# Both feed-forward blocks multiply by Strassen's scheme, with weight and token sums on VectorE

## The reference

```python
def swiglu(h, w_gate, w_up, w_down):
    return (jax.nn.silu(h @ w_gate) * (h @ w_up)) @ w_down

x = x + g2 * swiglu(modulate(rms_norm(x, norm_ffn[i]), sh2, sc2),
                    ffn_w_gate[i], ffn_w_up[i], ffn_w_down[i])     # i = 0, 1
```

## Time and profile before

| | before |
|---|---|
| median of 3 runs, us | 3224.8 |
| lowest and highest run, us | 3221.25, 3227.31 |
| profiled execution, us | 3226.9 |
| TensorE busy | 3013.9 us, 93% |
| VectorE, ScalarE, GpSimd busy | 1004.6, 646.0, 1067.1 us |
| matmul records in the gate and up products, two blocks | 1408 |
| matmul records in the down products, two blocks | 704 |

### The profile page before, as it was taken

One profiled execution on the slowest core, in us unless ns is written; L12 is line 12 of the kernel. 1 busy time (PEld: TensorE's weight loads), 2 busy tenths in 40 slices (PEclk: granted clock), 3 DMA queues, 4 the chain that ended last, 5 costly groups with the idle time before them and its releaser, 6 DMA issues.

```text
span 3226.9 us, 27822 instructions
## 1 busy us (share of the span) xinstructions
PE 3013.9 (93%) x10207; PEld 1660.1 (51%) x10207; DVE 1004.6 (31%) x2078; ACT 646.0 (20%) x1454; POOL 1067.1 (33%) x574
## 2 busy tenths in 40 slices
PE   7899999999999999997888969999999999999997
PEld 5455555476656644654556555444444444444443
DVE  6333455304455523335444164100000222100001
ACT  2132233113333412313322122100000100100000
POOL 5781681086460018608800000582000780000000
PEclk7899999989999999998889989999999999999999
DMA  7341341253321024313200101343222452222222
GB/s 240 103 127 62 114 126 45 85 147 85 85 79 33 27 83 121 103 59 108 72 17 26 52 1 39 122 156 96 71 75 78 140 159 65 78 78 71 73 72 71
DMA packets 267621, 278.07 MB, mean 86 GB/s; under 512 B 39379, under 2 KB 240352, under 8 KB 267392
## 3 DMA queue, kind: packets, MB, share of 16 engines
q1 hardware_dynamic: 238528, 175.56, 18.0%
q0 software_dynamic: 28224, 100.86, 10.2%
q10 hardware_dynamic: 768, 0.30, 0.0%
HBM read 274.59 MB, written 2.10 MB: 86 GB/s over the span
## 4 chain that ended last, share of the span: by engine, by line
PE 86%; DVE 7%; ACT 2%; DMA 2%; issue 2%; POOL 1%; SPq 1%; DVEq 0%; ACTq 0%; POOLq 0%
PE psum L683 44%; PE psum L831 10%; PE psum L1283 9%; PE psum L1118 2%; PE psum L710 2%; PE psum L805 2%; PE psum L1149 2%; PE psum L1104 2%; PE psum L725 2%; PE psum L817 1%; PE psum L1154 1%; PE psum L955 1%; PE psum L956 1%; DVE probs L2022 1%; DVE row_max L1988 1%
## 5 line engine op out<-in xcount | busy, mean ns | idle before, releaser
L683 PE MATMUL psum<-h,ring 128*128 128x512 f32 (+1 forms) x3216 | 1393.7, 594 | 33.4 <-ACT h L1416 27.3
L683 PEld LDWEIGHTS psum<-h,ring 128*128 128x128 f32 x3216 | 617.5, 194 | 771.8 <-issue 757.1
L610 POOL DMA_DIRECT2D ada_ring<-in_ada_w x192 | 115.1, 599 | 1574.7 <-DVE gains L1907 1361.4
L622 POOL TENSOR_SCALAR ada_ring<-ada_ring,cond 128x1024 f32<-128x1024 f32 x168 | 479.3, 2853 | 9.5 <-POOL ada_sum L626 1.8
L626 POOL TENSOR_TENSOR ada_sum<-ada_sum,ada_ring 128x1024 f32<-128x1024 f32 x168 | 394.9, 2350 | 14.9
L831 PE MATMUL psum<-og,ring 128*128 128x512 f32 x768 | 333.1, 593 | 2.3 <-DVE og L2440 2.0
L1283 PE MATMUL psum<-arena,ring 128*128 128x512 f32 x704 | 302.5, 592 | 0.0
L831 PEld LDWEIGHTS psum<-og,ring 128*128 128x128 f32 x768 | 144.6, 190 | 181.8 <-issue 178.3
L1283 PEld LDWEIGHTS psum<-arena,ring 128*128 128x128 f32 x704 | 133.8, 190 | 168.4 <-issue 168.4
L2450 DVE TENSOR_TENSOR arena<-psum,arena 128x512 f32 x44 | 30.4, 691 | 573.7 <-PE psum L683 573.7
L2069 DVE SCALAR_TENSOR_TENSOR x<-psum,mods,x 128x512 f32<-128x512 f32 x64 | 48.0, 751 | 481.9 <-PE psum L1283 272.2
(11 more groups left out here) (294 smaller groups left out, 2752.2 us busy)
## 6 DMA issues: line engine op xcount, KB each, us to landing
ada_ring<-in_ada_w POOLq DMA_DIRECT2D x192, 512.0 KB, 4.0
ring<-in_ffn_w_gate SPq DMA_DIRECT2D x22, 1024.0 KB, 5.3
ring<-in_ffn_w_up SPq DMA_DIRECT2D x22, 1024.0 KB, 5.3
ring<-in_ffn_w_down SPq DMA_DIRECT2D x32, 704.0 KB, 4.6
ring<-in_sc_w_in SPq DMA_DIRECT2D x12, 1024.0 KB, 6.6
ring<-in_mla_w_in SPq DMA_DIRECT2D x10, 1024.0 KB, 6.2
ring<-in_mla_w_out SPq DMA_DIRECT2D x8, 1024.0 KB, 5.2
ring<-in_swa_w_in SPq DMA_DIRECT2D x16, 512.0 KB, 5.3
```

What stands on the lines that cost most here:

```text
L610: pool.dma_start(ada_ring[:, i % 2, :], w[k * P:(k + 1) * P, first(part)]).then_inc(arrived[i % 2], n.give(f"ada_in{i % 2}", 16))
L622: step = nc.gpsimd.tensor_scalar(piece, ada_ring[:, i % 2, :], c, None, ALU.mult)
L683: m = pe.matmul(tile.at[:, part], lhs(k), rhs(k), start=(k == 0), stop=(k == K - 1))
```

## The change

Both blocks multiply by Winograd's form of Strassen's scheme. In a product each operand is seen as 2 x 2 quarters: the weights a11, a12 (the second half of the summed features), a21 (the second 128 output features), a22 (both), the tokens b11, b12 (the later 256 tokens), b21 (the second half of the summed features), b22 (both). Seven products of half width, called p1 to p7, take the place of eight:

- p1 = a11 b11, p2 = a12 b21, p6 = s2 t2, p5 = s1 t1, p7 = s3 t3, p3 = s4 b22 and p4 = a22 t4, in the order in which TensorE runs them (`first_parts`, `other_parts`). s1 to s4 are four sums of weight quarters, t1 to t4 four of token quarters. Each part is m accumulating matmuls of 128x128 by 128x256; m is 4 for gate and up, and 4, 4 and 3 for the three chunks into which the hidden tiles are cut for the down product.
- The parts of a slot go into three banks, and several of them build on one another in a bank. Between them ScalarE copies what a bank holds (`snaps`, after p1, p6 and p5) and VectorE adds such a copy and a bank (after p2, p7 and p3). For the down product VectorE adds each partial result straight to x, seven times a chunk (`add_chunk`).
- VectorE makes the sums of weights for each slot from the ring (`sum_weights`, four tensor_tensor of 128x(128 m)), once its transfer has landed and before TensorE comes to the slot's third part. It makes the token sums once a block for h (four of 128x1024) and once for each of the three chunks of hidden tiles.
- The down weights are loaded as 12 slots of 2m x 256 columns instead of 16 of 11 x 128.
- The order at the block's start: the first two slots do p1 and p2 both before the other parts of either, slot_begun comes at the second slot's p6, and the last `result_squares` before a block gives one slot_begun more so that both slots are loaded. `add_result` of the layer before makes the first slot's sums ahead of its last tile.

```diff
+HALF = T // 2
+BANK_SETS = ((0, 1, 3), (5, 6, 7))
+DOWN_CHUNKS = ((0, 4), (8, 4), (16, 3))
+PARTS_DONE = ((1, 2, 3, 4, 5, 6, 7), (8, 9, 10, 11, 12, 13, 14))
+FIRST_PARTS_DONE = ((1, 2, 5, 6, 7, 8, 9), (3, 4, 10, 11, 12, 13, 14))
...
-                    halves = [down[s * 11 * P:(s + 1) * 11 * P].rearrange("(k p) n -> p k n", p=P) for s in range(2)]
-                    for c in range(KT):
-                        for s in range(2):
-                            load((lambda slot: slot[:, 0:11 * P].rearrange("p (k n) -> p k n", n=P),
-                                  halves[s][:, :, c * P:c * P + P]))
+                    for pair in range(KT // 2):
+                        for first, m in DOWN_CHUNKS:
+                            load((lambda slot: slot[:, 0:2 * m * 256].rearrange("p (k n) -> p k n", n=256),
+                                  rows_of(down)[:, first:first + 2 * m, 256 * pair:256 * pair + 256]))
...
+                added = pe.matmul(SB[0], ones, sq_sum[:, :], start=True, stop=False, skip_group_check=True)
+                if frees_slot:
+                    added.then_inc(S["slot_begun"], n.give("slot_begun"))
...
+            def part(out, weights, moving, m, begins, slot_begins=False, fresh=None):
+                for k in range(m):
+                    if fresh is not None:
+                        pe.wait_ge(S["h_ready"], fresh + k + 1)
+                    last = pe.matmul(out, weights[:, k, :], moving[:, k, :], start=begins and k == 0, stop=True,
+                                     skip_group_check=True)
+                    if k == 0 and slot_begins:
+                        last.then_inc(S["slot_begun"], n.give("slot_begun"))
+                last.then_inc(S["part_done"], n.give("part_done"))
...
+            def first_parts(c, slot_begins=True, fresh=None):
+                b11, b12, b21, b22 = c.moving
+                part(c.banks[0], c.a11, b11, c.m, True, slot_begins=slot_begins, fresh=fresh)
+                part(c.banks[2], c.a12, b21, c.m, True, fresh=None if fresh is None else fresh + c.m)
+            def other_parts(c, moving_ready=None, slot_begins=False):
+                b11, b12, b21, b22 = c.moving
+                t1, t2, t3, t4 = c.sums
+                s1, s2, s3, s4 = c.w
+                pe.wait_ge(S["weights_summed"], n.take("weights_summed"))
+                if moving_ready is not None:
+                    pe.wait_ge(S["moving_summed"], moving_ready)
+                pe.wait_ge(S["snap_read"], c.snapped(1))
+                part(c.banks[0], s2, t2, c.m, False, slot_begins=slot_begins)
+                part(c.banks[1], s1, t1, c.m, True)
+                pe.wait_ge(S["snap_read"], c.snapped(2))
+                part(c.banks[0], s3, t3, c.m, False)
+                pe.wait_ge(S["snap_read"], c.snapped(3))
+                part(c.banks[1], s4, b22, c.m, False)
+                if moving_ready is not None:
+                    pe.wait_ge(S["moving_summed"], moving_ready + 1)
+                pe.wait_ge(S["sum_read"], c.summed(2))
+                part(c.banks[0], c.a22, t4, c.m, False)
...
             def ffn(job):
...
+                chunks = [Chunk(open_slot(), 4, i, moving, moving_sum, lambda k, i=i: snap0 + 4 * i + k,
+                                lambda k, i=i: sum0 + 3 * i + k) for i in range(2)]
+                first_parts(chunks[0], slot_begins=False, fresh=h0)
+                first_parts(chunks[1], slot_begins=False)
+                other_parts(chunks[0], moving_ready=t0 + 3)
+                other_parts(chunks[1], slot_begins=True)
...
+                with turns(pe, FT // 2 - 1, n, {"slot_full0": 16, "slot_full1": 16, "slot_begun": 2, "part_done": 14,
+                                                "weights_summed": 2, "snap_read": 7, "sum_read": 7}):
+                    snap_at, sum_at = n.of["snap_read"], n.of["sum_read"]
                     for i in range(2):
...
+                for pair in range(KT // 2):
+                    for at, (first, m) in enumerate(DOWN_CHUNKS):
+                        i = (3 * pair + at) % 2
+                        snap_at, sum_at = n.of["snap_read"].at, n.of["sum_read"].at
+                        pe.wait_ge(S["snap_read"], snap_at - 3)
+                        pe.wait_ge(S["sum_read"], sum_at - 4)
+                        if pair == 0:
+                            pe.wait_ge(S["hid_ready"], hid0 + (first + 2 * m) // 2)
+                        hid = ffn_hid[:, first:first + 2 * m, :]
+                        t2, t3, t4 = [v[:, 0:m, :] for v in hid_sum[at]]
+                        c = Chunk(open_slot(), m, i, halves_of(hid, m), (hid[:, 0:m, late], t2, t3, t4),
+                                  lambda k: snap_at + k, lambda k: sum_at + k)
+                        first_parts(c)
+                        other_parts(c, moving_ready=t0 + 4 * at + 3 if pair == 0 else None)
...
+                def turn(parts_done):
+                    at, summed = n.of["part_done"], n.of["sum_read"]
                     for i in range(2):
-                        tile = next_tile()
-                        done(tile)
-                        nc.scalar.activation(ffn_sig[:, i, :], tile.at, ACT.Silu).then_inc(tile_used[tile.bank], 1)
-                    skip(2)
-                squares_of_result()
+                        p1, p2, p6, p5, p7, p3, p4 = parts_done[i]
+                        r1, r2, r3 = [psum[:, b, early] for b in BANK_SETS[i]]
+                        for snap, (part, bank) in enumerate(((p1, r1), (p6, r1), (p5, r2))):
+                            act.wait_ge(S["part_done"], at.now(part))
+                            nc.scalar.activation(snaps[i][snap], bank, ACT.Copy).then_inc(S["snap_read"], n.give("snap_read"))
+                        if i == 0:
+                            act.wait_ge(S["sum_read"], summed.now(2))
+                            nc.scalar.activation(ffn_sig[:, 1, late], ffn_sig[:, 1, late], ACT.Silu)
+                            act.wait_ge(S["sum_read"], summed.now(3))
+                            nc.scalar.activation(ffn_sig[:, 0, :], ffn_sig[:, 0, :], ACT.Silu)
+                            act.wait_ge(S["part_done"], at.now(p4))
+                            nc.scalar.activation(ffn_sig[:, 1, early], r1, ACT.Silu).then_inc(S["snap_read"], n.give("snap_read"))
...
+            def sum_weights(i, m, steps=range(4)):
+                p = weight_slot[0] % 2
+                if 0 in steps:
+                    dve.wait_ge(S[f"slot_full{p}"], n.take(f"slot_full{p}", 16))
+                a11, a12, a21, a22 = quarters_of(ring[:, p], m)
+                s1, s2, s3, s4 = sums_of(weight_sum[i], m)
+                for step in steps:
+                    if step == 0:
+                        nc.vector.tensor_tensor(s1, a21, a22, ALU.add).then_inc(S["dve_step"], n.give("dve_step"))
+                    elif step == 1:
+                        nc.vector.tensor_tensor(s3, a11, a21, ALU.subtract)
+                    elif step == 2:
+                        dve.wait_ge(S["dve_step"], n.now("dve_step"))
+                        settle(nc.vector.tensor_tensor(s2, s1, a11, ALU.subtract))
+                    else:
+                        nc.vector.tensor_tensor(s4, a12, s2, ALU.subtract).then_inc(S["weights_summed"],
+                                                                                   n.give("weights_summed"))
+                        weight_slot[0] += 1
...
+            def first_weights_of(job):
+                weight_slot[0], n.of["slot_full0"].at, n.of["slot_full1"].at = MARK["ffn", job]
+                sum_weights(0, 4)
...
+            def gated_pair(hid, parts_done, between, first=False):
+                at, snapped = n.of["part_done"], n.of["snap_read"]
+                for i in range(2):
+                    p1, p2, p6, p5, p7, p3, p4 = parts_done[i]
+                    r1, r2, r3 = [psum[:, b, early] for b in BANK_SETS[i]]
+                    put = hid if i else [ffn_sig[:, q, :] for q in range(2)]
+                    if first and i == 0:
+                        sum_weights(1, 4)
+                    if not first and i == 0:
+                        dve.wait_ge(S["hid_ready"], n.now("hid_ready"))
+                    dve.wait_ge(S["part_done"], at.now(p2))
+                    dve.wait_ge(S["snap_read"], snapped.now(4 * i + 1))
+                    nc.vector.tensor_tensor(put[0][:, early], r3, snaps[i][0], ALU.add).then_inc(S["sum_read"], n.give("sum_read"))
+                    if i or not first:
+                        sum_weights(1 - i, 4)
+                    dve.wait_ge(S["part_done"], at.now(p7))
+                    dve.wait_ge(S["snap_read"], snapped.now(4 * i + 3))
+                    nc.vector.tensor_tensor(put[1][:, late], r1, snaps[i][2], ALU.add).then_inc(S["sum_read"], n.give("sum_read"))
+                    dve.wait_ge(S["part_done"], at.now(p3))
```

(64 more changed lines are left out.)

132 lines of the change are left out of this document (92 added, 40 removed).

## The result

The changed kernel takes 3148.3 us (median of 4 runs, 3146.9 to 3154.2) against 3223.9 before (4 runs beside them, 3221.3 to 3227.3): a ratio of 0.9765, 95% interval 0.975 to 0.9779. That is 75.6 us less; the forecast was 68 less, 3157 us. The spans of the profiled executions differ by 81.0: 3226.9 and 3145.9.

The account below looks back on a forecast made before the run. The number and width of TensorE's passes were taken to bound the feed-forward blocks. The terms -109 + 23 + 12.8 + 2.5 + 3 = -68 us took 3224.8 to 3157 us, range 3118 to 3200 (0.81).

Parts of the forecast that it names:

- The products: Feed-forward matmuls: 1848 half-width passes a block at 0.2157 us, 401.4 us with slow start, saving 109 us over both blocks.
- The rival of unhidden loads: TensorE's weight loads in series add at most 0.149 us to each of 3696 passes: 3705 us, chance 0.01.
- The quiet slots: Gate and up slots away from GpSimd: p4's chain ends 1.2 us early, so a slot costs only its products.
- Rival (b): VectorE's chain rules quiet slots too, with late links in the down product: 3175 to 3218 us, chance 0.17.
- late links in the down product: Down product: VectorE's order fits, forecast nothing; late, up to 2 us a chunk, 24 a block, 48 in all.
- Beside GpSimd: First block's loop: the chain takes 12.9 us, p4 waits 2.5 in each of 9 slots, 23 us in all.
- four sums that begin at any phase of this: VectorE's sums beside GpSimd: closed 1.6 us after each issue and 2.35 per tensor_tensor, they take 5.4 us in the mean.
- First two slots: Each block's start: quiet wait 2.3, beside GpSimd 6.0 plus 2.5, ScalarE's copy 1 a block; 12.8 us for both.
- The term of 2.5: First block's start beside GpSimd: VectorE reads p7 of the first slot about 2.5 us late, behind token sums and sum_weights.
- Clock: The 9 waiting slots beside GpSimd: half speed delays only p4 there, 3 us, ends 0 and 15.
- Rival (c): Slower: small gaps at seven hand-overs a slot lower TensorE's clock to 0.88, products cost 109 more: 3266 us, chance 0.09.
- Tail: Blocks' ends: the last square's matmul and first column sums hide no longer, 1.7 and 0.8 us, 2.5 together.

Follow-up runs that it names:

- e5: The changed kernel with one more all-SBUF VectorE addition of 1536 columns ahead of the weight sums of every slot but the first: 3210.1 us, ratio 0.9939.
- e1: The changed kernel with VectorE's read of the bank after p7 moved ahead of the sums of the next slot's weights: 3123.2 us, ratio 0.9683.
- e2: The changed kernel without VectorE's weight sums except for each block's first two slots: 3121.1 us, ratio 0.9677.
- e6: The changed kernel with two additional 1536-column VectorE additions ahead of the weight sums of every slot but the first: 3302.5 us, ratio 1.0221.
- e8: The changed kernel with the read of p7 ahead of the weight sums, plus one extra 1536-column VectorE addition per slot but the first: 3145.4 us, ratio 0.9752.

## Why the prediction was right, and where it was not

**The products.** Right. From p3 to p4 in the quiet slot is (2802.92 - 2801.20)/8 = 0.215 us a pass, and the down run of the first block took 133.1 us, forecast 133. A block without waits is 403 us, forecast 401.4 plus 1 for ScalarE's copy. The rival of unhidden loads is out; the streaming hides them throughout. (Its 3705 is 3 short of its own sum, 3157 + 551.)

**The quiet slots.** Right: 12.09 us a slot, chain and slack as worked out (1.2 forecast; in e5 1.8 us of extra work made a quiet slot 0.68 longer in the mean, so 1.1 was there). Rival (b) is out, and so are its late links in the down product.

**Beside GpSimd: right mechanism, term too large.** Forecast 23 us over nine slots. Nine slots waited, until 2201, for 11.6 us. The landing was as priced, 5.7 and 6.7 us for gate and up. The sums were not. Groups of VectorE's four sums from 2045 to 2205 us, the kernel after:

```profile
L2579 DVE TENSOR_TENSOR arena<-ring 128x512 f32<-128x512 f32 x11 | 16.3, 1483 | 32.6 <-DMA ring<-in_ffn_w_gate 16.7 <-DMA ring<-in_ffn_w_up 16.0
L2581 DVE TENSOR_TENSOR arena<-ring 128x512 f32<-128x512 f32 x11 | 10.6, 960 | 0.0
L2584 DVE TENSOR_TENSOR arena<-arena,ring 128x512 f32<-128x512 f32 x11 | 10.6, 960 | 0.0
L2586 DVE TENSOR_TENSOR arena<-ring,arena 128x512 f32<-128x512 f32 x11 | 10.3, 935 | 0.4
```

The means add to 4.3 us; less the overlap of the records (2.62 for 2.75 in the quiet slot) they take 4.2 where 5.4 was put, 3.0 to 5.9 in the nine slots. The step that failed is "four sums that begin at any phase of this": it let every stretch of GpSimd close to every sum, whichever of the two engines comes first. The last of the nine slots shows what happens (GpSimd issued its last transfer 6 us before):

```profile
2196.81 2.84 POOL L648 TENSOR_SCALAR ada_ring<-ada_ring,cond 128x1024 f32<-128x1024 f32 x1 [0.23 <-POOL ada_sum L652]
2197.35 1.11 DVE L2579 TENSOR_TENSOR arena<-ring 128x512 f32<-128x512 f32 x1 [3.27 <-DMA ring<-in_ffn_w_up]
2198.39 0.68 DVE L2581 TENSOR_TENSOR arena<-ring 128x512 f32<-128x512 f32 x1
...
2199.70 0.69 DVE L2586 TENSOR_TENSOR arena<-ring,arena 128x512 f32<-128x512 f32 x1
2199.74 2.87 POOL L652 TENSOR_TENSOR ada_sum<-ada_sum,ada_ring 128x1024 f32<-128x1024 f32 x1
```

The first sum is held and ends 1.65 us after the tensor_scalar began; the next go through at 0.68 beside the same tensor_scalar; the last starts 0.04 ahead of GpSimd's addition, which is then the one to take longer, 2.87 us for 2.34. In five of the nine slots only the first sum is held and the addition gives way like this. So what the forecast took for 1.6 us closed after each issue holds without an issue too: it is the first 1.0 us of the tensor_scalar, which otherwise starts 0.65 after the issue (a held sum then takes its own 0.69). With 4.2 in the place of 5.4 the forecast's own chain gives 11.7, a wait of 1.3, and 11.6/9 = 1.3 was measured.

The Trainium skill ("SBUF — State Buffer", SBUF: two separate sides) says why it goes both ways: VectorE and GpSimd contend for one pair of ports, and whichever issues first holds it for its whole instruction. The stretched operations of both engines agree for GpSimd's addition: held sums end 2.9 us after it began, 0.55 behind its own end. For its tensor_scalar the trace differs: it held sums for its first 1.0 us, not for its whole 2.85, and those that began later took 0.68.

**What a wait costs.** Missed. A slot that shows 1.16 us of wait is 13.51 long, not 13.24; each wait costs 0.27 more than its record, since the record of the matmul before it ends 0.16 late and eight passes after it take 1.99 instead of 1.89. Ten waits in the first block: 2.7 us.

**First two slots.** Forecast 9.5 and 3.3 us, measured 4.35 + 0.84 and 2.50 + 0.84, and 0.27 for each. The quiet 2.3 and the copy's 1 were near. The 6.0 beside GpSimd was 4.35, since that transfer landed in 5.4 us (6.3 put) and its sums took 4.8 (5.4 put). The term of 2.5, VectorE late at p7 of the first slot, was nothing: VectorE stood idle for 1.72 us before that read. The sums ahead of it took 3.5 us where 5.4 was put, and TensorE was late itself, since its first 32 passes ran in part at half speed (granted clock 0.73) and took 9.66 us where 6.9 is full speed. The token sums were forecast as the trouble and this slow start was not weighed against them.

**Clock.** Forecast 3, measured 4.8 in the first block (twice 1.8 in p4, 0.8 and 0.5 in the products behind it) and 1.5 in the second. Within the slots half speed came only after the waits of 4.35, 4.43 and 2.50, not after those up to 1.44. Rival (c) is out: the seven hand-overs of a slot leave the granted clock at 1.00 over the quiet stretches.

**Tail.** Forecast 1.7 and 0.8, measured 1.4 and 0.5. The timeline at the end of the first down run, against the earlier trace rows:

```profile
2468.72 0.48 DVE L2656 SCALAR_TENSOR_TENSOR x<-psum,mods,x 128x256 f32<-128x256 f32 x1 [0.81 <-PE psum L1302]
2469.12 0.68 DVE L2684 TENSOR_TENSOR sq_sum<-sq_sum,sq 128x512 f32<-128x512 f32 x1
...
2469.95 1.10 PE L764 MATMUL psum<-sq_sum,cst 128*128 128x512 f32 x2 [1.27 <-DVE sq_sum L2684]
```

**The sum.** First block: 402.9 without waits for VectorE, + 16.0 + 2.7 + 4.8 = 426.4, measured 426.1. Forecast 437, 11 more: the loop's waits were 11.4 less, the first pair's 4.3 less, the clock and the 0.27 after each wait 4.5 more. Second block: forecast 405, measured 406.5. So the blocks saved 79.4 where the forecast's terms for them give 109 - 23 - 12.8 - 3 = 70; the total came as near as it did because 15.7 us of waits too many stood against 4.5 us of after-effects too few. Of the 81.0 between the profiled executions the blocks and the tail make 77.5; the other 3.5 lie outside both, and no run shows them to be the change's: the start of the first block, ahead of which the changed kernel, e1, e2, e5 and e6 are the same, lay between 2038 and 2054 us in their profiled executions. Behind the first block's tail the changed kernel even lost 2.0 us: the next 40 products of its column sums took 6.97 us at a granted clock of 0.62, before 4.92 at 0.90, in e1 4.52 at 0.99.

## What to carry to other kernels

A loop that trades TensorE passes for VectorE work is judged by the one read that TensorE waits for: put it ahead of any work that depends on a transfer (e1 against the changed kernel 25 us, e8 against e5 65 us), and then more of VectorE's work costs nothing in the quiet and a third as much beside GpSimd (22 us against 62). Slack that is 1 us wide in the quiet is none beside GpSimd, where an added VectorE operation of 1.8 us with two SBUF inputs made waits of some 6; ask which of the two engines starts first, and how long the string of operations is.

## What the runs showed of the hardware

Beside GpSimd's job a string of four additions on VectorE took 3.0 to 5.9 us instead of 2.62, and a longer string lost more (e5: 7.2 to 9.1 for 4.41). Which of the four is held depends on where GpSimd stands as the string begins: in the changed kernel mostly the first (mean 1.48 us, the others 0.94 to 0.96), in e1, where the strings begin elsewhere, mostly the last. Groups of e1 from 2045 to 2205 us:

```profile
L2586 DVE TENSOR_TENSOR arena<-ring,arena 128x512 f32<-128x512 f32 x13 | 20.3, 1560 | 0.4
L2579 DVE TENSOR_TENSOR arena<-ring 128x512 f32<-128x512 f32 x13 | 12.4, 956 | 0.4 <-DMA ring<-in_ffn_w_gate 0.4
```

GpSimd's tensor_tensor held a sum until 2.9 us after its own start and its tensor_scalar until 1.65 to 1.67 after (later by as much as VectorE had first delayed it), the sum's own 0.69 included; later sums ran beside the tensor_scalar at 0.68. In some slots a sum that began up to 0.4 us ahead of the tensor_scalar, while GpSimd issued a transfer, was held to the same point (2124.59, 2.07 us); whether the issue does that no run tells. In the slots of all runs TensorE ran some or all of the next passes at 1.2 GHz after each wait of 2.5 us and more (up to 9.6 in e6), after some of 1.9 to 2.4 (1.86 and 2.02 in e6) and not after others (1.90 and 2.25 in e6, 2.39 in e8), and after none of 1.85 and less. One such fall cost 0.4 to 1.8 us in the eight passes right behind the wait, and up to 1.3 in the sixteen behind them.
